# Split-precision products in the layer tails, a reordered split schedule, token halves at stage ends, and rotary angles and masks moved into FFN2

## What is computed

```python
def token_mix(h, ...):                       # once in each of the two layers
    hq, hf, hi, hgate, cq, ckv, kr, gates = split(h @ w_in)
    o_a = rmsnorm(hgrn2_mix(hq, hf, hi, lb)) * silu(hgate)
    y_a = o_a @ w_br_a                       # 256x512 @ 512x1024
    y_b = mla_mix(cq, ckv, kr, pos, ...) @ w_br_b   # 256x512 @ 512x1024
    merged = sigmoid(g_a) * y_a + sigmoid(g_b) * y_b
    return merged @ w_out                    # 256x1024 @ 1024x1024
# x = x + g1 * token_mix(...);  x = x + g2 * grouped_moe(...)
# first block: x = x + 0.5 * (silu(a) * b) @ w_ffn_out, twice
```

## Time and profile before

| | |
|---|---|
| median of three runs | 1878.26 us |
| profiled execution | 1880.98 us, span 1879.3 us |
| PE busy | 1698.4 us, 90% |
| DVE busy | 1185.3 us, 63% |
| ACT busy | 975.1 us, 52% |
| mean granted TensorE clock | 0.948 |

### The profile page before, as it was taken

The page is one execution under the profiler, slowest core; times in us unless marked ns, Lnnn a source line. Parts: engine busy times, 40 slices in busy tenths (PEclk is TensorE's granted clock), DMA queues, the critical chain, the costliest instruction groups (busy, mean ns, idle before and its releaser), DMA issues.

```text
span 1879.3 us, 26700 instructions
## 1 busy us (share of the span) xinstructions
PE 1698.4 (90%) x10028; PEld 1407.5 (75%) x10028; DVE 1185.3 (63%) x1669; ACT 975.1 (52%) x1365; POOL 26.7 (1%) x58
## 2 busy tenths in 40 slices
PE   6999896999996989886899999969898769999995
PEld 6999794499995968743688888869694357888884
DVE  5544355455446454623788888854683377888886
ACT  4444334154444433401788888844451058888883
POOL 2000000000000000001000000000000010000000
PEclk9999998999998999987899999989999879999998
DMA  8555488745552569622398998935432218898992
GB/s 260 194 182 181 154 255 279 260 149 193 186 180 89 162 220 348 237 90 90 114 334 315 333 333 316 330 115 161 136 128 82 104 45 297 315 332 319 330 335 72
DMA packets 245831, 401.83 MB, mean 214 GB/s; under 512 B 6522, under 2 KB 151596, under 8 KB 245756
## 3 DMA queue, kind: packets, MB, share of 16 engines
q1 hardware_dynamic: 244792, 398.77, 61.6%
q0 software_dynamic: 592, 0.93, 0.2%
q10 hardware_dynamic: 372, 1.07, 0.2%
HBM read 399.70 MB, written 1.05 MB: 213 GB/s over the span
## 4 chain that ended last, share of the span: by engine, by line
PE 82%; DVE 11%; ACT 4%; issue 2%; DMA 1%; ACTq 0%; DVEq 0%
PE bank L1233 19%; PE bank L1175 14%; PE bank L1257 10%; PE bank L1104 8%; PE bank L1082 7%; PE bank L1188 6%; PE bank L1070 4%; PE bank L1269 3%; PE bank L1340 2%; DMA sb_ring<-in_w_in 1%; PE bank L1516 1%; DVE sb_w_lo L1818 1%; DVE sb_w_lo L1883 1%; PE bank L1093 1%; PE bank L1589 1%
## 5 line engine op out<-in xcount | busy, mean ns | idle before, releaser
L1883 DVE TENSOR_TENSOR sb_w_lo<-sb_ring,sb_moe_hi 128x1024 fp32r<-128x1024 f32 x384 | 448.4, 1220 | 30.8 <-ACT sb_moe_hi L700 30.6
L700 ACT ACTIVATE sb_moe_hi<-sb_ring 128x1024 fp32r<-128x1024 f32 x384 | 381.8, 1056 | 68.1 <-PE bank L1257 36.0
L1839 DVE TENSOR_TENSOR sb_w_lo<-sb_ring,sb_w_hi 128x1024 fp32r<-128x1024 f32 x128 | 151.1, 1222 | 171.6 <-ACT sb_w_hi L655 171.6
L655 ACT ACTIVATE sb_w_hi<-sb_ring 128x1024 fp32r<-128x1024 f32 x128 | 128.5, 1051 | 144.6 <-PE bank L1175 131.1
L1175 PE MATMUL bank<-sb_hT_hi,sb_w_hi 128*128 128x256 f32 x704 | 200.5, 285 | 3.3 <-DVE sb_hT_lo L1795 3.3
L1175 PE MATMUL bank<-sb_hT_lo,sb_w_hi 128*128 128x256 f32 x704 | 200.2, 284 | 0.0
L1175 PE MATMUL bank<-sb_hT_hi,sb_w_lo 128*128 128x256 f32 x704 | 200.1, 284 | 0.0
L1233 PE MATMUL bank<-sb_moe_hi,sb_xw_hi 128*128 128x512 f32 x480 | 194.2, 405 | 0.0
L1233 PE MATMUL bank<-sb_w_lo,sb_xw_hi 128*128 128x512 f32 x480 | 191.5, 399 | 0.0
L1233 PE MATMUL bank<-sb_moe_hi,sb_xw_lo 128*128 128x512 f32 x480 | 191.0, 398 | 0.0
L1257 PE MATMUL bank<-sb_moe_hi,sb_hid_hi 128*128 128x512 f32 x512 | 145.4, 395 | 2.9 <-DVE sb_hid_hi L1909 2.9
(11 more groups left out here) (465 smaller groups left out, 3135.7 us busy)
## 6 DMA issues: line engine op xcount, KB each, us to landing
sb_ring<-in_w_up SPq DMA_DIRECT2D x64, 1024.0 KB, 5.3
sb_ring<-in_w_gate SPq DMA_DIRECT2D x64, 1024.0 KB, 5.3
sb_ring<-in_w_down SPq DMA_DIRECT2D x64, 1024.0 KB, 4.9
sb_ring<-in_ada_w SPq DMA_DIRECT2D x48, 1024.0 KB, 7.5
sb_ring<-in_w_in SPq DMA_DIRECT2D x46, 1024.0 KB, 5.4
sb_ring<-in_ffn_w_in SPq DMA_DIRECT2D x44, 1024.0 KB, 5.0
sb_ring<-in_ffn_w_out SPq DMA_DIRECT2D x22, 1024.0 KB, 4.9
sb_ring<-in_w_out SPq DMA_DIRECT2D x12, 1024.0 KB, 5.0
```

Source lines behind the costliest of these rows:

```text
L655: A(w_hi[:, q % 2, c], ring[:, (pos0 + q) % RING, c], ACT.Copy).then_inc(s["w_hi"], 1)
L700: A(moe_hi[:, q % 3, c], ring[:, at % RING, c], ACT.Copy).then_inc(s["moe_hi"], 1)
L1839: ins = tt(w_lo[:, slot, c], ring[:, slot, c], w_hi[:, q % 2, c].bitcast(F32), ALU.subtract)
L1883: ins = tt(w_lo[:, slot, c], ring[:, slot, c], moe_hi[:, q % 3, c].bitcast(F32), ALU.subtract)
```

## The change

1. **Layer tails as split products.** `rows_product` is replaced in the layers by `rows_parts`: 24 fp32r matmuls to a tile. The eight tail tiles join the list of split tiles, so ACT rounds each and DVE makes each remainder. The activations are split as well: `ymT`, `oaT` and `mergedT` each get a rounded part (ACT) and a remainder (DVE).
2. **Schedule.** The splits come in the order `br_b0, br_b1, w_out0, w_out1, br_a0, br_a1, w_out2, w_out3`, which is not the order in which PE uses the tiles. `w_out0` and `w_out1` get buffers of their own (`tail_hi`). PE does `second_pT(0)` and `second_pT(1)` before the product of attT and vh, waits for `oa_rows` and `ymT_lo` ahead of `br_b0`, for `oaT_lo` ahead of `br_a0`, and does `gate_rows` between `w_out1` and `w_out2`. The banks of branch and transposes are exchanged.
3. **Token halves.** The last tile of FFN1, FFN2, the mixer's output, `br_a1`, `w_out3` and the last expert is done for token half 0 first, and a signal (`acc_half`, `br_half`) lets DVE work on half 0 while PE does half 1.
4. **Constants.** `before_layers()` becomes `rope_angles()` and `level_masks()`; DVE runs them in FFN2, after step 1 and after step 2 of the loop. POOL makes the patterns after the mixer's update of x.
5. Several semaphores are merged (`h_act`, `h_dve`, `mla_turned`, `mla_qk`) without other effect on the order, and `ada_rows` moves in memory.

```diff
+TAIL = ("br_b0", "br_b1", "w_out0", "w_out1", "br_a0", "br_a1", "w_out2", "w_out3")
...
+            def rows_parts(name, l_parts, out, start, stop, half_done=None):
+                w = (ring_tile(mix_hi(name).unsqueeze(1), 0, 1024), ring_tile(w_lo, place[name], 1024))
+                pe.wait_ge(s["mix_lo"], split_no[name] + 1)
+                for t in range(T):
+                    for kk in range(2):
+                        for m, (hp, wp) in enumerate(PARTS):
+                            for half in range(2):
+                                ins = mm(out[2 * t + half][:, :], l_parts[hp][:, kk, t * P:(t + 1) * P],
+                                         w[wp][:, kk, half * 512:(half + 1) * 512], ...)
+                    if half_done and t == 0:
+                        ins.then_inc(s[half_done], 1)
+                ins.then_inc(tiles_used, 1)
...
 PE, tail
+                pe.wait_ge(s["oa_rows"], run)
+                pe.wait_ge(s["ymT_lo"], run)
+                for n in range(2):
+                    rows_parts(f"br_b{n}.{l}", ..., bank[4:8], n == 0, n == 1)
+                    if n == 0:
+                        (transposes of oa into bank 2 and 3)
+                pe.wait_ge(s["oaT_lo"], run)
+                for n in range(2):
+                    rows_parts(f"br_a{n}.{l}", ..., acc, n == 0, n == 1, "br_half" if n else None)
+                (transposes of merged into bank 4 to 7)
+                for n in range(4):
+                    pe.wait_ge(s["mT_dve"], 4 * l + n + 1)
+                    rows_parts(f"w_out{n}.{l}", ..., acc, n == 0, n == 3, "acc_half" if n == 3 else None)
+                    if n == 1:
+                        pe.wait_ge(s["mT_dve"], 4 * l + 3)
+                        gate_rows(2 * l + 1)
...
 ACT, tail
+                    elif n == 7:
+                        split(f"br_b0.{l}", after=f"gates6.{l}")
...
+                split(f"br_b1.{l}", after=f"gates7.{l}")
                 root(next(roots))
                 act.wait_ge(s["mla_pv"], run)
                 (ymT, rounded)
+                act.wait_ge(s["hg_o"], run)
+                for n in range(2):
+                    split(f"w_out{n}.{l}", after=f"gates7.{l}")
+                act.wait_ge(s["oaT_out"], run)
+                A(oaT_parts[0][:, :, :], oaT[:, :, :], ACT.Copy).then_inc(s["oaT_hi"], 1)
+                for name, after in (("br_a0", "br_b0"), ("br_a1", "br_b1"), ("w_out2", "br_a0")):
+                    split(f"{name}.{l}", after=f"{after}.{l}")
+                (mergedT rounded, all eight pieces)
+                split(f"w_out3.{l}", after=f"br_a1.{l}")
...
 DVE, tail, in this order
                 (attT copy)
+                v.wait_ge(s["mla_pT"], 3 * l + 3); (two copies of attention weights); split(f"br_b0.{l}")
                 v.wait_ge(s["hg_o"], run); (oa scaled, squared, summed, root, multiplied); modulation(1) if l == 0
+                v.wait_ge(s["ymT"], run); (ymT remainder, two of 128x512); split(f"br_b1.{l}")
                 v.wait_ge(s["oaT"], run); (oaT, four of 128x256)
+                v.wait_ge(s["oaT_hi"], run); (oaT remainder, 128x1024)
+                split(f"w_out0.{l}"); split(f"w_out1.{l}"); split(f"br_a0.{l}")
+                gate_diag(l, 16)
                 used(f"br_b1.{l}"); (xn, four of 128x512)
+                split(f"br_a1.{l}")
+                t = 0: wait br_half; t = 1: used(f"br_a1.{l}"); (merged)
+                (mergedT remainders, eight of 128x256)
+                split(f"w_out2.{l}"); gate_copy(2 * l + 1, 0.5); split(f"w_out3.{l}")
+                add_gated_to_x(lambda: used(f"w_out3.{l}"))
...
 DVE, FFN2
                 for c in range(1, j0):          # j0 is 3
                     step(0, c)
+                    if c <= len(between):
+                        between[c - 1]()        # rope_angles, level_masks
```

More of the change, by code:

```diff
@@ L406, in mix_hi @@
         def mix_hi(name):
+            if name[:6] in ("w_out0", "w_out1") and "." in name:
+                return tail_hi[:, int(name[5]), :]
             buf = proj_hi if "." in name else w_hi
@@ L1095, in mem_product, with rows_product @@
                 ins.then_inc(tiles_used, 1)
-            def rows_product(pos, lhs, out, start, stop, i=0):
+            def rows_product(pos, lhs, out, start, stop, i=0, half_done=None):
                 landed(pos, i)
                 w = slot_view(pos, 1024)
-                for kk in range(2):
-                    for t in range(T):
+                for t in range(T):
+                    for kk in range(2):
                         for half in range(2):
@@ L1265, in scatter @@
                     pe.wait_ge(s["ye_lo"], i + (NE * l + e + 1))
-                    for hl in range(2):
-                        for t in range(T):
+                    for t in range(T):
+                        for hl in range(2):
                             for half in range(2):
@@ L1270, in scatter @@
                                          start=first and hl == 0, stop=last and hl == 1)
+                        if last and t == 0:
+                            ins.then_inc(s["acc_half"], 1)
                     ins.then_inc(s["scattered"], 1)
@@ L1963, in sparse, with add_to_x @@
                 ye_low(NE - 1)
-                v.wait_ge(s["scattered"], NE * (l + 1))
-            def add_to_x(scale, out=acc):
+            halves = [0]
+            def add_to_x(scale, whole_done, out=acc):
+                halves[0] += 1
                 for t in range(T):
+                    if t:
+                        whole_done()
+                    else:
+                        v.wait_ge(s["acc_half"], halves[0])
                     for half in range(2):
@@ L2365, in _ @@
                 cp(attT[:, 2], bank[4][:, :].rearrange("p (h c) -> p h c", h=HGH)).then_inc(s["level_added"], 1)
+                v.wait_ge(s["mla_pT"], 3 * l + 3)
+                for b in range(2):
+                    ins = cp(pT_second[:, 4 + 2 * b:6 + 2 * b], T_BANK[b][:, :].rearrange("p (h a c) -> p h a c", h=2, a=T))
+                ins.then_inc(s["pT_dve"], 1)
+                split(f"br_b0.{l}")
                 v.wait_ge(s["hg_o"], run)
@@ L2383, in _ @@
                     modulation(1)
-                v.wait_ge(s["hgate"], run)
+                v.wait_ge(s["ymT"], run)
+                for n in range(2):
+                    ins = tt(ymT_parts[1][:, 2 * n:2 * n + 2, :], two[n], ymT_parts[0][:, 2 * n:2 * n + 2, :].bitcast(F32),
+                             ALU.subtract)
+                ins.then_inc(s["ymT_lo"], 1)
+                split(f"br_b1.{l}")
+                v.wait_ge(s["h_act"], 3 * l + 2)
                 v.wait_ge(s["oaT"], run)
                 for h in range(HGH):
-                    ins = stt(oaT[:, h, :], bank[4 + h // 2][:, (h % 2) * SEQ:(h % 2 + 1) * SEQ], col("hgn", 4 * l + h),
+                    ins = stt(oaT[:, h, :], bank[2 + h // 2][:, (h % 2) * SEQ:(h % 2 + 1) * SEQ], col("hgn", 4 * l + h),
                               hgate[:, h, :], M, M)
                 ins.then_inc(s["oaT_out"], 1)
+                v.wait_ge(s["oaT_hi"], run)
+                tt(oaT_parts[1][:, :, :], oaT[:, :, :], oaT_parts[0][:, :, :].bitcast(F32), ALU.subtract).then_inc(s["oaT_lo"], 1)
+                split(f"w_out0.{l}")
+                split(f"w_out1.{l}")
+                split(f"br_a0.{l}")
+                gate_diag(l, 16)
                 v.wait_ge(s["oaT_out"], run)
```

248 lines of the change are left out of this document (131 added, 117 removed).

## The result

The changed kernel took 1848.43 us, against 1878.49 for the kernel before beside it (medians): ratio 0.9846, 95% interval 0.9816 to 0.9877. The median counts a fourth, disturbed run of 6109.82 us that the ratio leaves out; the others took 1844.77, 1845.74 and 1851.13. A second measurement (e9) gave 1849.59 and 0.9859 (0.9836 to 0.9883). The forecast was 1846 within 1833 to 1862, and faster: that is what came. My terms add up to 32.2 us of gain. By the ratios it was 29 us in the first measurement and 26 in the second; the two profiled executions (1880.98 and 1845.74 us) lie 35.2 apart.

What follows compares the result with a forecast made beforehand. PE, busy 90% of the span, was taken as the bound nearly everywhere. Tails -17.6, halves elsewhere -7.9, constants -11.9 and +5.2 sum to -32.2 us: 1848.8 from the profiled 1880.98, less 2.7 to the median, 1846; range 1833 to 1862.

Steps and rivals of the forecast that it cites:

- The tails' order: Layer tails: PE waits 5.5 us ahead of `br_b0`, 5.4 ahead of `br_a0`; `w_out0` starts 4.4 us after `br_a1`.
- covers: Layer tails: splits of `br_a1`, `w_out2`, `w_out3` are hidden under PE's work, the first by 1.7 us, the last by 1.8.
- Rival A: New tails gain nothing, since PE waits for DVE in more places: 17.6 us lost, 1864 us; chance 0.15.
- Rival B: Clock stays up in the new tails despite their gaps: 13.2 us more gain, 1833 us; chance 0.13.
- Rival D: Half clock through both tails: 82 us more than charged, 1928 us; decides from 39% of that; chance 0.05.
- term -17.6: Both layer tails, from cheaper split products and token halves less DVE waits and clock charges: 17.6 us gained.
- clock charges: Layer tails: 2.2 us on top for lower granted clock behind each of three gaps per layer.
- Halves: Ends of stages outside the tails: DVE's half 0 runs under PE's second half, 7.9 us gained.
- mixer's 1.1: End of the mixer: x's half 1 follows 1.25 us earlier, ACT's square and root move too; about 1.1 us gained.
- Constants: Angles and masks moved from layer 0's start into FFN2: 11.9 us gained there, 5.2 us lost in FFN2.
- Hole: Start of layer 0: PE's 9.3 us standstill and 2.6 us of slower tiles behind it go, 11.9 us gained.
- Rival C: Masks hold up FFN2 for their whole 8.85 us, so moving constants gains nothing: 1852 to 1853 us; chance 0.07.

Runs made afterwards that it cites:

- e9: The changed kernel measured once more, unedited, against the kernel before: 1849.59 us, ratio 0.9859.
- e1: Changed kernel with DVE's splits of `w_out0` and `w_out1` moved right behind that of `br_b1`: 1836.54 us, ratio 0.9786 to the kernel before.
- e2: Changed kernel with `ymT` rounded ahead of the root of `oa`'s norm and its remainders made during DVE's wait for that root: 1840.31 us, ratio 0.9817.
- e5: Kernel before plus the change's token halves and constants, the tails' products left in plain fp32 and old order: 1855.36 us, ratio 0.9895.
- e11: The kernel of e8 without its needless matmuls: 1824.12 us, ratio 0.9726 to the kernel before.
- e8: Changed kernel with tail splits, `ymT`, ACT's copy and `gate_diag` reordered, constants in six pieces, needless matmuls in gaps: 1815.30 us, ratio 0.9682.
- e6: Changed kernel with each sum onto x waiting for the whole last tile, as before: 1858.26 us, ratio 0.9907 to the kernel before.
- e4: Changed kernel with five needless fp32 matmuls in each gap ahead of `br_b0` and `br_a0`: 1840.05 us, ratio 0.9798 to the kernel before.

## Why the prediction was right, and where it was not

**The tails' order: right.** Gap ahead of `br_b0` 5.43 us (5.5), ahead of `br_a0` 5.64 (5.4), `w_out0` 4.6 us behind `br_a1` (4.4), `merged` and the covers of `br_a1`, `w_out2` and `w_out3` as walked through: PE waited for none of them. e1 shows that the second gap was the order of DVE's splits, e2 that the first was the norm's chain. **Rival A** is out by e5. **Rival B** would have had the clock up: it was at 0.50 behind two of three gaps in layer 0 and behind all three in layer 1. **Rival D** needed 39% of the tails' work at half clock; the lower clock took 5.7 us in layer 0 and 6.3 in layer 1, of some 48 that half clock throughout would have taken in each. The Trainium skill, "TensorE: Matmul & The Clock Gate", section HAM oscillation, describes a loop in which each wait brings the rate down and the next work starts slow. The trace after has that for five gaps of six (all but the 0.2 below), and the clock came back each time before the tile was done. That a kernel can lose more by this than it saves was my own conclusion and is not said there; no run here shows it.

**The tails' price: mis-sized.** The term -17.6 took the tails of before from one execution, at the clock that they had in it. Against them e5 shows the same code about 5 us faster (84.3 + 82.7 against 89.4 + 87.5, less 5 for the halves), at a higher granted clock. Each kernel has one trace here, so that this was the luck of one execution is likely and not shown; e11 and `q_up` show such differences behind equal gaps. Without the halves my term was 12.5; the traces show 7.5 and the medians 7. The profiled execution of before was among its slower ones; I took off 2.7 us for that, but the kernel before ran from 1870 to 1885 beside the later kernels, with medians of 1873 to 1875. The clock charges, 2.2 us three times in each tail, came to 2.7, 2.8 and 0.2 in layer 0, and 1.9, 2.6 and 1.9 in layer 1: 12 in all for 13.2: right in sum, not gap by gap. The missed wait, ACT's copy behind `split(br_b0)`, may be part of layer 1's 0.8 us of shortfall; e8 takes it out, but together with much else.

**Halves: right** where DVE was the last (FFN2 1.9 for 1.95, tails 2.6 and 2.5), and about right in the expert stages (2.4 forecast; e6 is 2.7 and 1.9 over the changed kernel there, and over all traces the cuts are 367.7 to 370.2 us without halves, 363.6 to 368.1 with). **The mixer's 1.1 failed**: ACT's square stands behind `ada_rows`, which comes with the last tile. FFN1, taken at nothing, may have given 0.5 (cuts at 210.0 to 211.2 with halves, 211.1 and 211.6 without). e6 puts the whole, the tails' own included, at 9 to 11 us, for 12.9; 1.1 of the difference is the mixer, the rest is open.

**Constants: the two terms right, the net not measured as such.** Hole 11.2 (11.9), FFN2 5.2 in the chain (5.2), about 6 by the cuts. Net 6.7 became 2.3 in the means of 19 runs, and 2.5 to 4.5 in the traces up to the cross level, where a slower `q_up` without the hole hides another 1.7 to 3.0: less that, 5.5 to 6.2 are left. **Rival C** wanted the masks' whole 8.85 us lost in FFN2; that did not happen. Whether the clock ahead of `q_up` falls more often when layer 0 starts without a hole stays open: three traces with and eleven without are too few.

So the total was hit in part by luck. The one term that was clearly too large is the tails', by 5 us for the two; what lies outside them came as added up (20 us in e5 for 19.6), though taken out one at a time, halves (9 to 11) and constants (2.3) give only 11 to 13 of it, and that difference stays open. The gain was 26 to 29 us by the ratios and not 32.2.

## What to carry to other kernels

When a supplier gets more work, look in its timeline for where it idles just ahead of the stretch in which it is late: here the order of two splits was worth 12 us, more than the cheaper products won in both tails (7). Work moved into slack (an engine's idle time) belongs there in pieces about as long as the idle time in front of each deadline, not in one lump of the right total. Before a difference of a few us is explained, compare the same, unchanged code in both traces: if it ran at two speeds, that part is the clock.

## What the hardware showed that I had not expected

Short gaps bring the clock down in some executions and not in others. Behind 2.46 to 2.50 us of idling the same tile ran at full speed or not: 8.63 and 7.10 us (before and e5, plain), 7.38 and 7.36 (e2), 5.76 and 7.13 (e11, layer 0 and layer 1). Behind 1.83 us `br_a0` and `br_a1` took 12.75 (e8), behind 1.82 us 11.18 (e11). Behind 2.02 us `q_up` took 8.0, 9.7 or 11.0 us in layer 0, and 9.7 in two of thirteen traces in layer 1. Behind the 28 gaps of 4.87 us and more, counted under e4, the tile was slow every time. Needless fp32 matmuls in a gap of 5.4 us kept the clock up for the work behind (5.73 us instead of 8.13, for 4.49 us of them, e4). And for some groups the loss comes in a few sizes only: `w_out0` and `w_out1`, 11.2 us at full clock behind their gap, took 12.7 to 12.8 or 14.1 otherwise; `br_b0` shows no such steps (7.2 to 8.6 behind the long gap).
